# Moving the opening's sums of squares, the first root and the spread q in a two-layer RWKV-7 / retention decoder step

## The reference

```
def _rmsnorm(x, g):
    y = x * rsqrt(mean(x * x, -1) + 1e-6)
    return y * g

def _layer(x, pos, s_wkv, s_ret, s_shift, p):
    h = _rmsnorm(x, norm_mix_pre)
    z = h @ w_in                               # 1024 x 6944
    za, zb, (ga, gb) = parts of z
    ya = _rwkv7_branch(za, ...)                # token shift: zs = za + mu * (prev - za), LoRAs, chunked delta rule
    q, k, v, gate = split(zb); q, k = rotary(q), rotary(k) / 8
    # per head and chunk:
    #   inner = (q k^T * d_in) v;  cross = (q S) * d_q;  S = S * d_c + (k * d_k)^T v
    yb = head_norm(inner + cross) * silu(gate)
    m = sigmoid(ga) * (ya @ w_out_a) + sigmoid(gb) * (yb @ w_out_b)
    x = x + _rmsnorm(m @ w_o, norm_mix_post)
    h = _rmsnorm(x, norm_ffn_pre)
    f = (silu(h @ w_ffn_gate) * (h @ w_ffn_up)) @ w_ffn_down
    x = x + _rmsnorm(f, norm_ffn_post)
```

## Time and profile before

| | us |
|---|---|
| median of 3 runs | 1342.22 |
| the profiled execution's own time | 1344.05 |
| its span in the trace | 1342.3 |
| PE busy | 1288.2 (96%) |
| DVE busy | 900.5 (67%) |
| ACT busy | 517.6 (39%) |

### The profile page before, as it was taken

The page is one execution under the profiler, slowest core; times in us unless marked ns, Lnnn a source line. Parts: engine busy times, 40 slices in busy tenths (PEclk is TensorE's granted clock), DMA queues, the critical chain, the costliest instruction groups (busy, mean ns, idle before and its releaser), DMA issues.

```text
span 1342.3 us, 27273 instructions
## 1 busy us (share of the span) xinstructions
PE 1288.2 (96%) x11888; PEld 1218.3 (91%) x11888; DVE 900.5 (67%) x1550; ACT 517.6 (39%) x737; POOL 14.7 (1%) x26
## 2 busy tenths in 40 slices
PE   6999999999998999999989999999999989999996
PEld 5899997889997999999878999978999979999996
DVE  3887768687776556653468876669776766656533
ACT  4553032445435433333445520233444354333432
POOL 0001000000000000000000020000000000000000
PEclk9999999999998999999989999999999989999998
DMA  5433123544443544544423322245443534444442
GB/s 203 142 108 132 41 92 120 182 151 156 142 144 123 169 154 145 156 145 155 142 74 119 125 97 68 81 143 192 141 144 130 167 114 136 149 151 148 154 145 71
DMA packets 51175, 179.49 MB, mean 134 GB/s; under 512 B 6256, under 2 KB 7024, under 8 KB 49776
## 3 DMA queue, kind: packets, MB, share of 16 engines
q1 hardware_dynamic: 41904, 150.49, 35.3%
q10 hardware_dynamic: 9152, 27.25, 5.9%
HBM read 166.57 MB, written 8.53 MB: 130 GB/s over the span
## 4 chain that ended last, share of the span: by engine, by line
PE 89%; DVE 5%; ACT 3%; DMA 1%; issue 1%; ACTq 0%; SPq 0%; DVEq 0%
PE dense L1138 51%; PE core L1138 38%; DVE w_lo L693 1%; ACT w_hi L438 1%; DVE x L741 1%; DVE y_out L739 1%; ACT L426 0%; DMA ret_s<-ret_t 0%; DMA x<-x_t 0%; DVE bonus L804 0%; DVE tmp L790 0%; DVE bonus L800 0%; PE core L1299 0%; DVE h_lo L697 0%; DVE zs L801 0%
## 5 line engine op out<-in xcount | busy, mean ns | idle before, releaser
L693 DVE TENSOR_TENSOR w_lo<-w_raw,w_hi 128x1024 fp32r<-128x1024 f32 x282 | 344.8, 1223 | 255.7 <-ACT w_hi L438 254.5
L438 ACT ACTIVATE w_hi<-w_raw 128x1024 fp32r<-128x1024 f32 x282 | 297.7, 1057 | 564.7 <-PE dense L1138 428.0
L1138 PE MATMUL dense<-h_hi,w_hi 128*128 128x320 f32 x1296 | 418.4, 323 | 26.1 <-DVE h_lo L697 14.6
L1138 PE MATMUL dense<-h_hi,w_lo 128*128 128x320 f32 x1296 | 405.7, 313 | 0.0
L1138 PE MATMUL dense<-h_lo,w_hi 128*128 128x320 f32 x1296 | 405.6, 313 | 0.0
L1138 PEld LDWEIGHTS dense<-h_hi,w_hi 128*128 128x128 f32 x1296 | 248.0, 191 | 43.4 <-issue 31.4
L1138 PEld LDWEIGHTS dense<-h_lo,w_hi 128*128 128x128 f32 x1296 | 248.4, 192 | 2.1
L1138 PEld LDWEIGHTS dense<-h_hi,w_lo 128*128 128x128 f32 x1296 | 248.1, 191 | 0.0
L1138 PE MATMUL core<-h_hi,w_hi 128*128 128x320 f32 x416 | 129.7, 312 | 4.2 <-DVE w_lo L693 4.2
L1138 PE MATMUL core<-h_hi,w_lo 128*128 128x320 f32 x416 | 129.0, 310 | 0.0
L1138 PE MATMUL core<-h_lo,w_hi 128*128 128x320 f32 x416 | 129.0, 310 | 0.0
(11 more groups left out here) (250 smaller groups left out, 1843.8 us busy)
## 6 DMA issues: line engine op xcount, KB each, us to landing
w_raw<-wts SPq DMA_DIRECT2D x282, 512.0 KB, 3.5
ret_t<-ret_t ACTq DMA_DIRECT2D x16, 256.0 KB, 4.0
ret_s<-ret_t ACTq DMA_DIRECT2D x16, 256.0 KB, 2.4
ret_rest<-ret_d ACTq DMA_DIRECT2D x2, 1536.0 KB, 7.8
qk_rot<-qk_raw ACTq DMA_DIRECT2D x8, 320.0 KB, 6.0
dmask<-rconst ACTq DMA_DIRECT2D x2, 1152.0 KB, 5.7
s_st<-wkv_st ACTq DMA_DIRECT2D x2, 1024.0 KB, 5.4
wkv_s<-s_st ACTq DMA_DIRECT2D x2, 1024.0 KB, 3.9
```

The lines of the kernel that those rows point to most:

```text
L438: act.activation(w_hi[n % RING][:, :], w_raw[n % RING][:, :], ACT.Copy).then_inc(hi_ready.sem, 1)
L693: dve.tensor_tensor(w_lo[r][:, :], w_raw[r][:, :], w_hi[r][:, :].bitcast(F32), ALU.subtract).then_inc(low_made.sem, 1)
L1138: return pe.matmul(out, lhsT, rhs, start=start, stop=stop)
```

## The change

Four things. Both groups of sums of squares stand in one place of the opening, before step 4 in layer 0 and before step 6 in layer 1 (`SUMS_AT`), with one wait for all eight squares; the strips are added one step later. ACT makes the root directly behind the copy, and the high part of tile 3 comes after the root. DVE makes the first `q_exp` in the tail, behind the last state update and ahead of the low part of tile 35; `make_qexp` itself is the same.

```diff
--- before.py
+++ after.py
@@ -27,6 +27,7 @@
 LN_EXP, SIGMOID, SILU = "natural_log_exp_and_others", "sigmoid_and_others", "silu_and_others"
 X_GROUPS = ((0, 1), (1, 2), (2, 4), (4, 6), (6, 8))
 FIRST_WEIGHTS = (0, 2, 3)
+SUMS_AT = (4, 6)
 X_GROUP_OF = [i for i, (a, b) in enumerate(X_GROUPS) for _ in range(a, b)]
 DECAY = float(np.exp(-0.5))
 RMS_EPS, EPS_A, EPS_B = 1e-6, 64e-5, 1e-5
@@ -482,13 +483,12 @@
                 def x_root(k):
                     act.wait_ge(*x_partial(layer, k))
                     act.activation(acc[:, :], core[0][:, 0:T], ACT.Copy).then_inc(x_parted.sem, 1)
-                    if k == 1:
-                        high(RING)
                     act.wait_ge(*x_summed(layer, k))
                     inverse_root(root[:, :], core[0][:, 0:T], 1.0 / D, eps(0)).then_inc(x_rooted.sem, 1)
 
 
                 x_root(1)
+                high(RING)
 
                 def za(j):
 
@@ -953,6 +953,13 @@
                     dve.wait_ge(*finished(layer, j))
                     dve.tensor_tensor(gate_of(j), bank(j)[:, 0:T], root[:, :], ALU.mult).then_inc(dense_evac_v.sem, 1)
 
+                def make_qexp(hp):
+
+                    q4 = bc(ch(qk_rot, hp, TP, T).rearrange("p (j t) -> p j t", j=4), 2, 4)
+                    m4 = bc(rc_small[:, R_QX - R_DQ:NRC - R_DQ].rearrange("p (a t) -> p a t", a=4), 1, 4)
+                    dve.tensor_tensor(q_exp[:, :].rearrange("p (j a t) -> p j a t", j=4, a=4), q4, m4, ALU.mult).then_inc(qexp_ready.sem, 1)
+                    dve.wait_ge(*qexp_ready(layer, hp + 1))
+
                 for what, i in TAIL:
                     if what == "gate":
                         gate(T_GATE + i)
@@ -965,18 +972,13 @@
                         dve.tensor_tensor(ch(sq_a, i), ch(y_a, i), ch(y_a, i), ALU.mult).then_inc(cent_a.sem, 1)
                         dve.wait_ge(*cent_a(layer, i + 1))
                         dve.scalar_tensor_tensor(ch(y_a, i), ch(y_a, i), vec("gna_g", i), ch(g_a, i), ALU.mult, ALU.mult).then_inc(y_gated.sem, 1)
+                    if (what, i) == ("s", 3):
+                        dve.wait_ge(*rcs_loaded(layer, 1))
+                        make_qexp(0)
                     if (what, i) in (("mean", 3), ("s", 3)):
                         low(layer, T_GATE + RING + (what == "s"))
                 low(layer, T_GATE + RING + 2)
 
-                def make_qexp(hp):
-
-                    q4 = bc(ch(qk_rot, hp, TP, T).rearrange("p (j t) -> p j t", j=4), 2, 4)
-                    m4 = bc(rc_small[:, R_QX - R_DQ:NRC - R_DQ].rearrange("p (a t) -> p a t", a=4), 1, 4)
-                    dve.tensor_tensor(q_exp[:, :].rearrange("p (j a t) -> p j a t", j=4, a=4), q4, m4, ALU.mult).then_inc(qexp_ready.sem, 1)
-                    dve.wait_ge(*qexp_ready(layer, hp + 1))
-                dve.wait_ge(*rcs_loaded(layer, 1))
-                make_qexp(0)
                 gate(T_GATE + 3)
                 dve.memset(sts[:, :], 0.0).then_inc(sts_clear.sem, 1)
                 dve.wait_ge(*sts_clear(layer, 1))
@@ -1173,9 +1175,9 @@
 
                 def x_sum(k, half):
 
+                    pe.wait_ge(*x_squared(layer, (k - 1) * KT + 4 * half + 4))
                     for j in range(4):
                         c = 4 * half + j
-                        pe.wait_ge(*x_squared(layer, (k - 1) * KT + c + 1))
                         ins = mm(core[0][32 * j:32 * j + 32, 0:T], ones[:, 0:32], ch(sq8, c), half == 0, half == 1)
                     if half:
                         ins.then_inc(x_partial.sem, 1)
@@ -1204,7 +1206,11 @@
                             if k == KT - 1:
                                 ins.then_inc(tile_used.sem, 1)
 
-                opening(0, 0, h_ready, 0, {4: lambda: x_sum(1, 0), 8: lambda: x_sum(1, 1), 10: lambda: x_pick(1)})
+                def sums():
+                    x_sum(1, 0)
+                    x_sum(1, 1)
+                at = SUMS_AT[layer > 0]
+                opening(0, 0, h_ready, 0, {at: sums, at + 1: lambda: x_pick(1)})
                 pe.wait_ge(*lora_loaded(layer, 1))
 
                 def lora_mm(n):
```

## The result

The changed kernel takes 1335.31 us, the median of five runs from 1332.84 to 1337.03, against 1342.27 (five runs from 1341.97 to 1343.23) for the kernel before on the same chip. The ratio is 0.9944 with an interval of 0.9932 to 0.9955: 7.0 us faster (6.0 to 9.1 by the interval), where 8.5 were forecast. The profiled execution took 1335.93 us for a span of 1334.0, against 1344.05 and 1342.3 before: 8.1 and 8.3 less. The five runs of the new kernel scatter over 4.2 us, those of the old one beside them over 1.3.

What follows compares the result with a forecast made beforehand. PE, busy for 96% of the span, was held to wait last for DVE's low part of a weight and q_exp; 5.1 (openings) + 3.4 (q_exp) = 8.5 us off the median 1342.22 gave 1333.7, range 1331.3 to 1337.3.

Steps and rivals of the forecast that it cites:

- The openings: PE's wait of 2.11 us before tile 3 goes whole in both layers: 2.6 and 2.5, together 5.1 us.
- The second group of sums: Opening: placed right behind the first group, it costs 0.54 us at full clock and 1.07 at 1.2 GHz.
- rival 5: Openings: behind eight sums PE stays at 1.2 GHz through the rest; 12.4 us lost against 8.5 gained, 1346.1; chance 0.02.
- Rival 4: Openings: PE next waits for the high part behind the root, 2 us of each wait stay; 1337.9; chance 0.05.
- q_exp: Made in DVE's idle time in the tail, it removes PE's 1.98 us wait at the cross term: 1.7 a layer, 3.4 both.
- new wait: At the second head pair's scores PE waits about 1.8 us for the state's updates at the end of DVE's chain.
- Rival 1: Retention: the clock falls again behind the new wait in one layer, 1.65 us given back, 1335.4; chance 0.25.
- the forecast's case: Retention: no new fall of the clock behind the new wait, 1333.7 us; chance 0.41.
- Rival 3: Slow stretches behind the norms end elsewhere; a 10 us one becoming 6.5 saves half of 3.5, 1332.0; chance 0.10.

Runs made afterwards that it cites:

- e1: The changed kernel again, no edit: 1334.05 us.
- e3: Changed kernel with the opening as before (sums apart, high part ahead of the root), only q_exp in the tail: 1341.33 us.
- e7: Changed kernel with both groups of sums before step 4 in layer 1 too, instead of step 6: 1334.34 us.
- e6: Changed kernel with sums and strips back in their old places (before steps 4, 8 and 10), root still ahead of the high part: 1342.54 us.
- e5: Changed kernel with the high part of tile 3 again ahead of the root on ACT, sums still together: 1336.16 us.
- e2: Changed kernel with q_exp put back behind the tail, the opening's changes kept: 1336.87 us.
- e4: Changed kernel with the last two pieces of y_a moved on DVE from ahead of the state's updates to behind the centring of the outputs: 1329.35 us.
- e8: Changed kernel with the last two pieces of y_a moved behind the centring and q_exp back behind the tail: 1336.25 us.
- e9: The changed kernel a third time, no edit: 1335.99 us.
- e10: Changed kernel with only the last piece of y_a (1.85 us of DVE) moved behind the centring of the first head pair: 1329.07 us.
- e11: Changed kernel with the last two pieces of y_a moved behind the centring, run again: 1330.75 us.

## Why the prediction was right, and where it was off

**The openings: right in mechanism and size.** 2.6 and 2.5 were forecast, 2.84 and 2.7 came. Some 0.4 of the 2.84 is luck: the first rise of the clock came about 0.8 us earlier in this profile than in that of before. The pair with like rises, e1 and e3, has 30.69 - 28.20 = 2.49. The second group of sums behind the first costs what one matmul of 320 fp32 columns costs: 2.35 - 1.30 = 1.05 at 1.2 GHz for the 1.07 taken, 1.28 - 0.75 = 0.53 at full clock for 0.54. The place of the first rise is a matter of the execution and not of the number of sums. With eight sums it came by 19.24 in the first profile, at 20.4 in e1, and during the sums in e7; with four it came at 19.64 before, at 20.2 in e3 and at 18.4 in e6. In none of the ten profiles with eight sums did PE stay at 1.2 GHz through the opening, so rival 5 falls. (Its price doesn't fit its sign either: 50 tile matmuls at 0.27 are a slow stretch of 13.5 us, not 8.5.) Rival 4 falls with the lines of layer 1 above, where the high part stands right behind the root and PE waits for nothing; e5 and e6 show that this holds as long as the sums are early.

**What 1.2 GHz cost in each kernel.** Each run comes with the mean clock granted to the core, c. The stretches of these traces are at full or at half clock, so a mean c over a time T cost (1 - c) x T, if PE was busy all that time. Two things limit this. Behind the norms PE partly wasn't busy, so it is an upper bound. And c leaves out the start of the execution, as this window of the kernel before shows (PE, PEld, DVE, ACT and POOL busy, then the granted clock):

```profile
0.00:19.00 19.00, 7.79 (x30) 6.07 (x31) 8.27 (x14) 10.84 (x20) 0.44 (x6) 1.00 0.86 298
```

It says 1.00, but within it the tile matmuls from 14.38 to 16.25 start 0.27 apart. What the first rise gives or takes is therefore in the rest and not in the cost. From the medians (c is the mean over the runs):

| kernel | runs | time | c | cost of 1.2 GHz | rest |
|---|---|---|---|---|---|
| the changed kernel, first result | 5 | 1335.31 | 0.9856 | 19.2 | 1316.1 |
| before, first group | 15 | 1342.99 | 0.9835 | 22.1 | 1320.9 |
| e1, the changed kernel | 5 | 1334.05 | 0.9864 | 18.1 | 1315.9 |
| e2, opening only | 5 | 1336.87 | 0.9846 | 20.6 | 1316.3 |
| e3, q_exp only | 11 | 1341.33 | 0.9848 | 20.4 | 1321.0 |
| e4, y_a late | 4 | 1329.35 | 0.9875 | 16.6 | 1312.7 |
| before, second group | 15 | 1342.5 | 0.9833 | 22.4 | 1320.1 |
| e5, high part first | 5 | 1336.16 | 0.9854 | 19.5 | 1316.7 |
| e6, sums apart | 11 | 1342.54 | 0.9846 | 20.6 | 1321.9 |
| e7, as changed | 5 | 1334.34 | 0.9856 | 19.2 | 1315.1 |
| e8, y_a late, q_exp old | 5 | 1336.25 | 0.9852 | 19.8 | 1316.5 |
| before, third group | 9 | 1342.29 | 0.9837 | 21.9 | 1320.4 |
| e9, the changed kernel | 5 | 1335.99 | 0.9844 | 20.8 | 1315.2 |
| e10, half of e4 | 4 | 1329.07 | 0.9875 | 16.6 | 1312.5 |
| e11, e4 again | 4 | 1330.75 | 0.9880 | 16.0 | 1314.8 |

How far this can be trusted is seen where one kernel stands in it more than once: the changed kernel's rest is 1316.1, 1315.9 and 1315.2 and its cost 18.1 to 20.8, and e4 and e11, also one kernel, have rests of 1312.7 and 1314.8. A difference of two lines is good to 1 or 2 us. Taking the openings back costs 7.3 us (e3 less e1): 2.2 by the clock and 5.1 in the rest, where positions on PE say some 5.5. With the sums apart it costs 8.2 (e6 less e7): 1.4 and 6.8, where positions say 5.5 and the two longer waits 0.8. So the openings give what was worked out. The 1.4 to 2.2 us of clock on top, which no term of the prediction held, point the same way twice but are no larger than the scatter of the table, so they aren't shown.

**q_exp: right in mechanism, too large in size.** The idle time at the cross term went, nothing was added on DVE, and the wait that took its place came at the place, from the instruction and with the length forecast. The mis-sized term is the 1.7 us a layer, 3.4 in all. It was worked out as 1.98 + 1.65 less a new wait of 1.8 to 1.9, on the assumption that the slow stretch behind q_exp's wait belonged to the kernel. It belongs to an execution. Both layers of the profile of before happened to have it, so the first two profiles give 28.31 - 26.55 = 1.76 a layer, as forecast, while the medians give 1.7 us (e3) and 2.8 (e2 less e1) for both layers. DVE's chain lets PE gain just what DVE itself gains by starting earlier, 0.42 + 0.20 = 0.62, and that is what the spacing shows where no slow stretch was there to remove (27.18 to 26.56, e2 to e1). With one it is 1.58 to 1.76. Over the profiles that stretch followed the wait for q_exp in 3 of 6 places (two before, one of two in e2, none in e8), and the new wait of 1.74 in 4 of 14 (one each in the changed kernel's first profile, e3, e6 and e9; none in e1, e5 and e7). An estimate from these counts, which are small: 0.62 and in 3 of 6 places 1.05 more, less 1.57 in 4 of 14, is 0.7 us a layer, 1.4 for both.

**The clock behind the new wait.** Rival 1, a fall in one layer, is what the first profile shows (0.54 in layer 0), and e9 too; e1 shows the forecast's case. Of which of them the median of five runs comes nearest is luck: the same kernel gave 1335.31, 1334.05 and 1335.99. The Trainium skill, page "TensorE: Matmul & The Clock Gate", section "What's actually happening", has the throttled state as the default that activity has to lift. Here the same wait of 1.74 us in the same program was followed by 1.2 GHz in some executions and by full speed in others, so it must be carried as a chance and not as a rule. The table says the same of the medians, as far as it reaches. q_exp's place brings 2.8 from e2 to e1, 2.5 of it by the clock, and 1.7 from before to e3, 1.7 of it by the clock; the rest, 0.4 and -0.1, lies below the 1.2 of the positions, within what such means can tell. With DVE's chain relieved (e8 to e4, of two groups) it is 6.9, 3.2 by the clock and 3.7 in the rest, near the two waits of 1.98; from e8 to e11 it is 5.5, 3.8 and 1.7.

**The sum.** 5.1 was forecast for the openings and 3.4 for q_exp. The three measurements of the changed kernel are 7.0, 8.9 and 6.3 us below the before beside them. In e1's group 5.0 of the 8.9 are in the rest and 4.0 in the clock. The positions on PE say 5.5 and 1.2 for what is no clock, 6.7. That the rest shows 1.7 less isn't settled, but two things that c doesn't hold move as much from profile to profile. One is the first rise: in the kernels with early sums it moves tile 3 from 26.60 (e7) to 28.20 (e1). The other lies between tile 3 and the first scores of layer 0, where no wait and no slow clock differs: it is 212.8 us in the first profile, e4, e9 and e10, but 213.7 in e7 and e11, 214.0 in e1 and 214.1 in e8. What makes the difference stays open. Rival 3, norms with shorter slow stretches, didn't come in the first profile: between the first rise and the output's norm the stretches at 1.2 GHz add up to 34 us before and 34 after. In e1 they are 27. Its price was too high in any case: the norm's stretch that grew from 6.8 to 10.2 us in layer 1 cost 0.5 at most, and the one that shrank by as much in layer 0 of e1 against the first profile gave 1.0, not 1.7.

**Where the rest lay.** The prediction named DVE's chain as the next bound and took 1.8 us as the price of standing behind it, which the runs confirm. It did not ask what on that chain could go elsewhere: y_a's last piece could (e10), and that is worth another 4.7 to 6.9 us in the medians (e4, e10 and e11), 3.1 of it in positions.

## What to carry to other kernels

When an instruction that ended a wait is made early, the gain is what the next chain lets through. Measure it start to start of a block in the timeline (here scores to scores), not by the wait that went away: 1.98 us of it vanished and 0.62 arrived, until the work on DVE that nobody was waiting for stood behind the work that PE waited for. An operation moved to the front of a queue pays only when its input is already there (e6), so move the producer first and the order second.

## What the runs showed that I had not expected

The same kernel's profiles differ in where PE runs at 1.2 GHz: behind a wait of 1.74 us in 4 of 14 cases for some 3.4 us, behind one of 1.98 in 3 of 6, and behind a norm for 6.8 or for 10.2 us. A stretch of 3.4 us behind the scores costs 1.57 (27.39 for 25.82 to the next scores); 3.4 us more behind a norm cost 0.5 to 1.0. The waits of 2.11 and 2.53 before tile 3, with tile matmuls on both sides, were followed by no slow stretch in any of their six places. The first five runs of the changed kernel follow their mean clock: 0.984 in those of 1335.93 and 1337.03, 0.985 in 1335.31, 0.987 in 1334.0, 0.988 in 1332.84. Its new waits don't change by more than 0.02 from profile to profile, so the scatter of 4 us is mostly the clock's. And the kernels with fewer waits were granted more of it: 0.9833 to 0.9837 in the three groups of before, 0.9844 to 0.9864 in the three of the changed kernel, 0.9875 to 0.9880 in e4, e10 and e11. So a removed wait can be worth more than its length; how much of it is the wait's doing these means don't tell.
